# The ends of three attentions reordered: high splits ahead of the copies, and group norms one group at a time

## The reference, cut to what matters

```python
ya = neighborhood_attention(qa, ka, va, rpb_na[l])
yb = sliding_window_attention(qb, kb, vb, sink_sw[l], t5_table)
yc = axial_attention(qc, kc, vc, gq_ax[l], gk_ax[l])
ga, gb, gc = split_cols(g_group[l], GROUP_WIDTHS)
y = jnp.concatenate([rms_norm_2(ya, ga), rms_norm_2(yb, gb), rms_norm_2(yc, gc)], axis=-1)
x = x + gt_a * (y @ w_o[l])
```

## Time and profile before

| | us |
|---|---|
| runs, median of 3 | 2042.83 (2037.96 to 2043.96) |
| profiled execution, its time | 2036.57 |
| its span | 2034.4 |
| TensorE busy | 1886.8 |
| VectorE busy | 1638.9 |
| ScalarE busy | 1137.1 |
| mean granted TensorE clock | 0.977 of full speed |

### The profile page before, as it was taken

One profiled execution on the slowest core, in us unless ns is written; L12 is line 12 of the kernel. 1 busy time (PEld: TensorE's weight loads), 2 busy tenths in 40 slices (PEclk: granted clock), 3 DMA queues, 4 the chain that ended last, 5 costly groups with the idle time before them and its releaser, 6 DMA issues.

```text
span 2034.4 us, 29285 instructions
## 1 busy us (share of the span) xinstructions
PE 1886.8 (93%) x9222; PEld 1560.4 (77%) x9222; DVE 1638.9 (81%) x2173; ACT 1137.1 (56%) x1616; POOL 36.1 (2%) x47
## 2 busy tenths in 40 slices
PE   1999999978899999999999999988799999789998
PEld 1987888867788888888888888866678887577886
DVE  6988886768898999998998989897776669677554
ACT  1435444443777777777777777654544444544443
POOL 2000000000000000000000000000000000000000
PEclk9999999989999999999999999988899999889999
DMA  8877996556699999999999999957468875745662
GB/s 293 338 256 272 346 362 213 150 167 213 201 364 339 368 335 372 330 353 349 343 356 340 363 340 363 337 192 223 139 211 269 272 245 149 249 136 178 217 218 73
DMA packets 368507, 551.08 MB, mean 271 GB/s; under 512 B 35860, under 2 KB 293143, under 8 KB 368375
## 3 DMA queue, kind: packets, MB, share of 16 engines
q1 hardware_dynamic: 365424, 547.81, 80.5%
q10 hardware_dynamic: 2118, 1.46, 0.3%
q0 software_dynamic: 832, 0.30, 0.1%
HBM read 548.38 MB, written 1.08 MB: 270 GB/s over the span
## 4 chain that ended last, share of the span: by engine, by line
PE 81%; DVE 11%; ACT 4%; issue 2%; DMA 2%; POOL 0%; SPq 0%; DVEq 0%; ACTq 0%; POOLq 0%
PE ps L402 24%; PE ps L404 24%; PE ps L403 23%; PE ps L891 2%; DVE units_low L397 2%; ACT prob L1253 2%; PE ps L1060 2%; PE ps L945 2%; DVE mod_acc L1561 1%; PE ps L878 1%; ACT units_high L393 1%; DVE x_tokens L1588 1%; DVE x_normed L1587 1%; DMA mod_in<-in_mod_w 1%; DMA mod_in<-in_w_mod 1%
## 5 line engine op out<-in xcount | busy, mean ns | idle before, releaser
L397 DVE TENSOR_TENSOR units_low<-raw_units,units_high 128x1024 fp32r<-128x1024 f32 (+2 forms) x840 | 982.8, 1220 | 113.4 <-ACT units_high L393 107.3
L393 ACT ACTIVATE units_high<-raw_units 128x1024 fp32r<-128x1024 f32 (+2 forms) x840 | 844.8, 1058 | 237.7 <-PE ps L404 217.8
L402 PE MATMUL ps<-units_high,hT_high 128*128 128x512 f32 (+2 forms) x1576 | 621.8, 395 | 8.3 <-DVE hT_low L1630 3.8
L404 PE MATMUL ps<-units_high,hT_low 128*128 128x512 f32 (+2 forms) x1576 | 617.5, 392 | 0.0
L403 PE MATMUL ps<-units_low,hT_high 128*128 128x512 f32 (+2 forms) x1576 | 614.1, 390 | 0.0
L402 PEld LDWEIGHTS ps<-units_high,hT_high 128*128 128x128 f32 (+1 forms) x1576 | 296.9, 188 | 75.0 <-issue 5.8
L404 PEld LDWEIGHTS ps<-units_high,hT_low 128*128 128x128 f32 (+1 forms) x1576 | 296.4, 188 | 66.0
L403 PEld LDWEIGHTS ps<-units_low,hT_high 128*128 128x128 f32 (+1 forms) x1576 | 296.6, 188 | 63.8 <-issue 0.2
L402 PE MATMUL ps<-units_high,aT_high 128*128 128x512 f32 x632 | 258.8, 409 | 1.2 <-DVE qkT L1798 0.6
L404 PE MATMUL ps<-units_high,aT_low 128*128 128x512 f32 x632 | 248.2, 393 | 0.0
L403 PE MATMUL ps<-units_low,aT_high 128*128 128x512 f32 x632 | 246.5, 390 | 0.0
(11 more groups left out here) (275 smaller groups left out, 1438.7 us busy)
## 6 DMA issues: line engine op xcount, KB each, us to landing
raw_units<-in_moe_w_gate SPq DMA_DIRECT2D x352, 256.0 KB, 4.6
raw_units<-in_moe_w_up SPq DMA_DIRECT2D x352, 256.0 KB, 5.8
raw_units<-in_moe_w_down SPq DMA_DIRECT2D x176, 512.0 KB, 6.4
mod_in<-in_mod_w SPq DMA_DIRECT2D x96, 512.0 KB, 5.8
mod_in<-in_w_mod SPq DMA_DIRECT2D x96, 512.0 KB, 5.3
raw_units<-in_w_gu SPq DMA_DIRECT2D x176, 256.0 KB, 3.5
raw_units<-in_w_down SPq DMA_DIRECT2D x44, 512.0 KB, 4.3
raw_units<-in_w_in SPq DMA_DIRECT2D x32, 512.0 KB, 6.8
```

Source lines behind the costliest of these rows:

```text
L393: eng.activation(whi[:rows, n % H, 0:width], raw[:rows, n % R, 0:width], ACT.Copy).then_inc(f.hi, 1)
L397: eng.tensor_tensor(low[:rows, n % R, 0:width], raw[:rows, n % R, 0:width], whi[:rows, n % H, 0:width].bitcast(F32), ALU.subtract).then_in ...
L402: pe.matmul(dst, ah, bh, start=start, stop=False, **kw)
L404: return pe.matmul(dst, al, bh, start=False, stop=stop, **kw)
```

## The change

It has two parts. In all three attentions ScalarE's high split of an output-weight unit moves from behind the copies of a pair to ahead of them. In the second and third attention the end is done group by group: the sink's exponential and the squares of the third group (heads 10 to 15) are put between the last pair's exponentials and its copies; heads 10 to 15 are scaled first, then 0 to 7, then 8 and 9; the roots of the first and third group are made in one chain, those of the middle group in a second one; the chunks of y are transposed in the order 0 1, 6 7, 2 3, 4 5, the last two pairs only behind the second unit of the projection, and the output weights are loaded in that order. TensorE waits for heads 10 to 15 to be scaled before it makes the product of head 8, which lies in the same PSUM bank.

```diff
@@ -438,6 +438,9 @@
     GROUPS = ((0, 256), (256, 640), (640, 1024))
+    G_AT = (0, 4, 2)
+    Y_PAIRS = [(0, 1, 2, 3, 4), (0, 3, 1, 2), (0, 3, 1, 2)]
+    Y_CHUNK = lambda a, c: 2 * Y_PAIRS[a][c // 2] + c % 2
 
@@ -566,7 +569,7 @@
                 bias_load(1 + l, nth)
-            phase(fb, n0 + N_WO2, 8, rows_of(g["w_o_2"][l]))
+            phase(fb, n0 + N_WO2, 8, lambda k: rows_of(g["w_o_2"][l])(Y_CHUNK(1 + l, k)))
             mods(HEAD_MODS[1 + l][0] + HEAD_MODS[1 + l][1])
@@ -768,6 +771,8 @@
 
+            if free is not None:
+                pe.wait_ge(*free)
             for k in range(chunks):
@@ -780,6 +785,8 @@
                     sum_gate(0)
+                if beside is not None and k == 1:
+                    beside()
             for t in range(T):
@@ -880,6 +887,8 @@
                     pe.wait_ge(s_pte, i0 + j + 1)
+                    if second and j == n - 2:
+                        pe.wait_ge(s_ho, 6 * (a - 1) + 2)
                     h = order[j]
@@ -893,16 +902,15 @@
 
-        def y_transposes(a):
+        def y_transposes(a, first, end):
 
             w = KR if a == 0 else P
-            chunks = W1 // KR if a == 0 else DC
-            for pair in range(chunks // 2):
+            for pair in range(first, end):
                 pe.wait_ge(s_y, Y_BEFORE[a] + Y_READY[a][pair])
                 if pair >= 4:
                     pe.wait_ge(s_yTl, 2 * YT0[a] + 2)
                 for i in range(2):
-                    c = 2 * pair + i
+                    c = Y_CHUNK(a, 2 * pair + i)
                     for t in range(T):
@@ -1140,8 +1148,9 @@
             attention(1 + l)
-            y_transposes(1 + l)
-            project_out(fb, n0 + N_WO2, DC, P, lambda k: (s_yTl, 2 * YT0[1 + l] + k + 1))
+            y_transposes(1 + l, 0, 2)
+            project_out(fb, n0 + N_WO2, DC, P, lambda k: (s_yTl, 2 * YT0[1 + l] + k + 1),
+                        free=(s_ho, 6 * (l + 1)), beside=lambda: y_transposes(1 + l, 2, 4))
             sum_cols(s + 1)
@@ -1253,6 +1262,10 @@
                                              bias=negm(qt, h), scale=-1.0, accum_out=sums(qt, h))
                     last.then_inc(s_exp, 1)
+                if p < AHEAD:
+                    split_high(ac, f, n_out + p, 0, rows)
+                if p == (n - 1) // 2 and ending is not None:
+                    ending()
                 for j in pair:
                     ac.wait_ge(s_ptp, i0 + j + 1)
@@ -1260,8 +1273,6 @@
                                   ps[:, 6 + j % 2, 0:w], ACT.Copy).then_inc(s_pte, 1)
-                if p < AHEAD:
-                    split_high(ac, f, n_out + p, 0, rows)
 
@@ -1465,18 +1475,26 @@
             transposed(3, 7)
-            attention(1 + l, fb, n0 + N_WO2)
-
-            ac.wait_ge(s_al, 2 + l)
-            ac.activation(ale[:, :, 0:6], ale[:, :, 0:6], ACT.Exp).then_inc(s_ale, 1)
-            for nth, (out_of, t, grp) in enumerate(((1, 0, 0), (2, 1, 0), (3, 0, 1), (3, 0, 2), (4, 1, 1))):
+            def group_square(t, grp, scaled):
                 c0, c1 = GROUPS[grp]
-                ac.wait_ge(s_ho, 4 * l + out_of)
-                ac.activation(qkT[:, 4 + 2 * nth:6 + 2 * nth, :].rearrange("p a b -> p (a b)")[:, 0:c1 - c0],
-                              xn[:, t, c0:c1], ACT.Square, scale=(c1 - c0) ** -0.5, accum_out=ssx[:, 0, 2 * grp + t:2 * grp + t + 1])\
-                    .then_inc(s_gsq, 1)
-            yT_high(1 + l)
-            highs(fb, n0 + N_WO2, AHEAD, 8)
+                ac.wait_ge(s_ho, 6 * l + scaled)
+                ac.activation(qkT[:, 4 * grp + 2 * t:4 * grp + 2 * t + 2, :].rearrange("p a b -> p (a b)")[:, 0:c1 - c0],
+                              xn[:, t, c0:c1], ACT.Square, scale=(c1 - c0) ** -0.5,
+                              accum_out=ssx[:, 0, G_AT[grp] + t:G_AT[grp] + t + 1]).then_inc(s_gsq, 1)
+
+            def sink_and_last_group():
+                ac.wait_ge(s_al, 2 + l)
+                ac.activation(ale[:, :, 0:6], ale[:, :, 0:6], ACT.Exp).then_inc(s_ale, 1)
+                for t in range(T):
+                    group_square(t, 2, 1 + t)
+
+            attention(1 + l, fb, n0 + N_WO2, ending=sink_and_last_group)
+            group_square(1, 0, 4)
+            group_square(0, 1, 5)
+            yT_high(1 + l, 0, 4)
+            highs(fb, n0 + N_WO2, AHEAD, AHEAD + 2)
+            yT_high(1 + l, 4, 8)
+            highs(fb, n0 + N_WO2, AHEAD + 2, 8)
             highs(fb, n0 + N_FFN2, 0, 3)
@@ -2131,20 +2148,51 @@
             link(ve.reciprocal(ale[:, :, :], xstat[:, 1, :, :]))
-            heads_out(1 + l, s_ho)
-            ve.wait_ge(s_ho, 4 * (l + 1))
-            c0, c1 = GROUPS[2]
-            link(ve.tensor_tensor_reduce(out=qkT[:, 0:2, :].rearrange("p a b -> p (a b)")[:, 0:c1 - c0],
-                                         in0=xn[:, 1, c0:c1], in1=xn[:, 1, c0:c1], scale=1.0 / (c1 - c0), scalar=0.0,
-                                         op0=ALU.mult, op1=ALU.add, accum_out=ssx[:, 0, 5:6]))
-            ve.wait_ge(s_gsq, 5 * (l + 1))
-            link(ve.tensor_scalar(ssx[:, 0, 0:6], ssx[:, 0, 0:6], EPS, None, ALU.add))
-            rsqrt(ssx[:, 0, 0:6], ssx[:, 1, 0:6], ssx[:, 2, 0:6], ssx[:, 3, 0:6])
-            for i, (c0, c1) in enumerate(GROUPS):
+
+            def heads_scaled(h0, h1):
+                last = max(HEAD_ORDER.index(h) for h in range(h0, h1))
+                ve.wait_ge(s_pv, HEADS_BEFORE[1 + l] + 1 + last)
                 for t in range(T):
-                    ve.tensor_scalar(xn[:, t, c0:c1], xn[:, t, c0:c1], ssx[:, 1, 2 * i + t:2 * i + t + 1], None,
-                                     ALU.mult).then_inc(s_y, 1)
-            yT_low(1 + l)
+                    at = (h0 % 8) * HD
+                    ve.tensor_tensor(
+                        xn[:, t, h0 * HD:h1 * HD].rearrange("p (h d) -> p h d", d=HD),
+                        ps[:, 2 * t + h0 // 8, at:at + (h1 - h0) * HD].rearrange("p (h d) -> p h d", d=HD),
+                        ale[:, t, h0:h1][:, :, None].broadcast_to((P, h1 - h0, HD)), ALU.mult).then_inc(s_ho, 1)
+
+            def group_square(t, grp):
+                c0, c1 = GROUPS[grp]
+                return ve.tensor_tensor_reduce(
+                    out=qkT[:, 4 * grp + 2 * t:4 * grp + 2 * t + 2, :].rearrange("p a b -> p (a b)")[:, 0:c1 - c0],
+                    in0=xn[:, t, c0:c1], in1=xn[:, t, c0:c1], scale=1.0 / (c1 - c0), scalar=0.0,
+                    op0=ALU.mult, op1=ALU.add, accum_out=ssx[:, 0, G_AT[grp] + t:G_AT[grp] + t + 1])
+
+            def group_roots(a, b):
+                link(ve.tensor_scalar(ssx[:, 0, a:b], ssx[:, 0, a:b], EPS, None, ALU.add))
+                rsqrt(ssx[:, 0, a:b], ssx[:, 1, a:b], ssx[:, 2, a:b], ssx[:, 3, a:b])
+
+            def group_normed(grp):
+                c0, c1 = GROUPS[grp]
+                for t in range(T):
+                    at = G_AT[grp] + t
+                    ve.tensor_scalar(xn[:, t, c0:c1], xn[:, t, c0:c1], ssx[:, 1, at:at + 1], None, ALU.mult)\
+                        .then_inc(s_y, 1)
+
+            heads_scaled(10, 16)
+            heads_scaled(0, 8)
+            ve.wait_ge(s_ho, 6 * l + 4)
+            link(group_square(0, 0))
+            ve.wait_ge(s_gsq, 4 * l + 3)
+            group_roots(0, 4)
+            group_normed(0)
+            heads_scaled(8, 10)
+            ve.wait_ge(s_ho, 6 * l + 6)
+            link(group_square(1, 1))
+            group_normed(2)
+            yT_low(1 + l, 0, 2)
+            ve.wait_ge(s_gsq, 4 * l + 4)
+            group_roots(4, 6)
+            group_normed(1)
+            yT_low(1 + l, 2, 4)
             for k in range(AHEAD, 8 + 3):
```

More of the change, by code:

```diff
@@ L756, in conv_in, with project_out @@
                 last.then_inc(fa.used, 1)
-        def project_out(f, n0, chunks, rows, ready, conv=False):
+        def project_out(f, n0, chunks, rows, ready, conv=False, free=None, beside=None):
             yTh, yTl = (v[:, :, :, :].rearrange("p a k s -> p (a k) s") for v in (aTh, aTl))
@@ L1015, in _ @@
         attention(0)
-        y_transposes(0)
+        y_transposes(0, 0, 5)
         project_out(fa, N_WO1, W1 // KR, KR, lambda k: (s_yTl, k + 1))
@@ L1239, in swiglu, with attention @@
                     hooks[j]()
-        def attention(a, f, n_out, rows=P):
+        def attention(a, f, n_out, rows=P, ending=None):
             second = a > 0
@@ L1272, in _, with yT_high @@
         YP0 = YT0
-        def yT_high(a):
+        def yT_high(a, first, end):
             w = KR if a == 0 else P
-            chunks = W1 // KR if a == 0 else DC
-            for c in range(chunks):
+            for c in range(first, end):
                 ac.wait_ge(s_yTp, YP0[a] + c // 2 + 1)
@@ L1282, in yT_high @@
                 else:
-                    gcol = V_GG + 8 * (a - 1) + c
+                    gcol = V_GG + 8 * (a - 1) + Y_CHUNK(a, c)
                     ac.activation(hTh[0:w, c, :], src, ACT.Copy, scale=cols[:, gcol:gcol + 1]).then_inc(s_yTh, 1)
@@ L1358, in _ @@
```

(9 more changed lines are left out.)

## The result

The changed kernel takes 2024.8 us (median of 4 runs, 2022.54 to 2026.55), the kernel before 2040.39 beside it (4 runs, 2037.84 to 2043.96): ratio 0.9922, 95% interval 0.9899 to 0.9944, 15.6 us faster between the medians. I forecast 2035.0 with a range from 2028.5: the side was right, the size half of what came. The profiled execution took 2026.55, 10.0 less than that of before. Single executions of one kernel differ by up to 13 us here, so times are compared by medians and ratios, and the profiles stretch by stretch.

The account below looks back on a forecast made before the run. The prediction took TensorE's dense products to bound most of the kernel, a serial chain the head-pair loops, and VectorE and TensorE almost level the end. Terms -12.4 and +4.6 gave -7.8, so 2035.0 us from 2042.83; range 2028.5 to 2041.5.

Parts of the forecast that it names:

- Part 1: Attention loops: the high split goes into ScalarE's idle time before the copies, 0.95 us sooner per pair; sum -12.4 us.
- rival (a): End of second and third attention: TensorE's clock stays up, tail costs 0.3 us instead of 2.4; total -11.9; chance 0.2.
- rival (d): Attention loops: more pairs run at half clock, 1.5 us dearer each; at eleven, +8.7, 2051.5 us; chance 0.07.
- The first pairs: Start of the loops: full 0.95 us gain in the first attention, nothing in the second, half in the third.
- Part 2: End of second and third attention by groups: projection 3.5 us sooner, residual 2.4 later (2.2 in the third); sum +4.6 us.
- (b): End of attentions: clock stays low through units 0 and 1, residual 5.2 us late; total -2.2, 2040.6 us; chance 0.13.
- (c): Attention loops: VectorE's maxima set the pace, part 1 gains perhaps half, 6.2 us; total -1.6, 2041.2 us; chance 0.1.
- The scale: Whole kernel: profiled 2036.57 us gave 2028.8; three timed runs' median, 2042.83, lay 6.3 above, so the forecast was 2035.0.

Follow-up runs that it names:

- e0: The changed kernel run again, nothing altered, against the kernel before: median 2024.31 us, ratio 0.9922.
- e2: The changed kernel with the high split put back behind the copies, leaving the end by groups alone: median 2044.30 us, ratio 1.0017 to the kernel before.
- e10: The changed kernel with the split put back behind the copies in the first attention alone: median 2031.91 us, ratio 0.9953 to the kernel before.
- e5_before_bridged: The kernel before, no split moved, with four extra products in TensorE's pause before a pair's transposes: median 2032.57 us, ratio 0.9970 to the kernel before.
- e1: The kernel before with nothing but the high split moved ahead of the copies: median 2023.57 us, ratio 0.9915 to the kernel before.
- e4: The changed kernel with two low splits and two modulation sums ahead of the second half of y's low parts: 2015.69 us, ratio 0.9881 to the kernel before.
- e6: e4 with eight extra products on TensorE between the scores of the first and second pair: median 2015.80 us, ratio 0.9892 to the kernel before.
- e7: e4 with extra products in TensorE's last two pauses of the second and third attention: median 2013.51 us, ratio 0.9877 to the kernel before.
- e8: e4 with the extra products of both e6 and e7: median 2012.14 us, ratio 0.9865 to the kernel before.
- e3: The changed kernel with one low split and one modulation sum ahead of the second half of y's low parts: 2019.02 us, ratio 0.9906 to the kernel before.

## Why the prediction was right or wrong

- **Part 1, -12.4: wrong in size, -17.3 measured.** The step that failed is "The difference, 0.95, is the split's place in the queue", taken as all that a moved split gives. The queue's share is right where it can be seen alone (81.2 to 72.7 us for nine splits). But I treated the clock of the loop as given. The earlier trace rows had it, 0.70 and a pair of 7.63 us, and I used them only against rival (a) and for rival (d), in which the clock gets worse; "Shorter pairs make TensorE denser, which speaks against it" was the start of the missing rival, in which it gets better. What the runs showed in its place: the move also keeps TensorE's clock up in the loops, and filling the pause alone, with no split moved, is worth 6.1 (3.5 to 8.6).
- **The first pairs** gave less than I counted: 12.4 less the 8.5 of the stretches is 3.9 for the first two pairs, and the seven profiles with the split ahead and nothing else changed there average 35.4 us (31.9 to 38.2) against 37.4 with it behind (36.9, 38.3, 37.2), about 2.0 with a scatter that is larger. 8.5 + 2.0 + 6.1 = 16.6 for 17.3 measured.
- **Part 2, +4.6: right in mechanism, +3.5 measured** (0.6 to 6.3). In the second attention each mark of the tail was hit within 0.7 us. What I had not counted is the half clock in the norm's transposes behind the residual (3.65 against 1.94); what I had counted too dear is the residual itself: over six old tails in the profiles it starts at +34.9 to +36.4 (mean 35.8), and I had only one, at +35.34, to compare with. Up to the feed-forward's input the six old tails take 45.8 on average and eight new ones with VectorE's order as changed and no extra products (two each of after, e0, e2 and e10) 47.4, so 1.6 a tail, 3.2 for two.
- **Rival (a)** did not happen in the second attention and in neither of e0_after's: products there start at 0.43. In the profile of the changed kernel the third attention had the clock up at its last pair (first product at +11.55, residual at +35.2), though its first products too start at 0.43. Made to happen, it gives 5.7 us for the two tails by the ratios (3.7 between the medians); I had 4.1. The rule of the Trainium skill that I cited there, TensorE: Matmul & The Clock Gate, "Why this matters for your kernels", asks for short pauses between bursts of matmuls. In direction the loop's rows agree (pauses of at most 0.7 us, with one of 1.03 in each first attention: 1.00 in every stretch; up to 1.6: 0.77 to 0.94), and I had weighed the rule only for the tail. But the section warns of pauses longer than these 1.6, so by it alone the loops before would have kept their clock; the measurement decides.
- **Rivals (b), (c), (d)** did not come: unit 1 runs at 0.23, VectorE waits before its maxima, and no loop stretch got slower.
- **The scale.** 2035.0 came from a median of 2042.83 of three runs. Over 17 runs it is 2039.8. That is 3 of the 10.2 us by which I missed; the other 7 are the sum, 5 of them part 1 and 1 part 2, and the last lies within what the runs can tell.

## What to carry to other kernels

Where a loop's profile shows TensorE's clock between its two levels, a change that shortens TensorE's pauses can get two gains, as here, the queue's and the clock's; price the second from the rows at either level, and give it a chance of its own as a gain. Before costing such a change, fill the pause with products whose result is not used: it costs one run and measures the clock's share with nothing moved. When work is started sooner on one engine, look at what the list of the other holds between the new waits: here reordering four operations was worth more (8.4) than the regrouping cost.

## What was unexpected of the hardware

- In the loop, with a pause of up to 1.6 us in each pair of 5.2 or 6.1, the clock was down part of the time, a different part in each execution (0.77, 0.87, 0.93 for the same stretch of the same instructions), while with the split ahead, and pauses of at most 0.7 (one of 1.03 in each first attention), all 29 such stretches of ten profiles show 1.00 and last 21.3 or 25.7 us to 0.02. Whether the scatter in time of the kernel before (2036.55 to 2046.95) comes from this isn't shown, and two things speak against its being all of it: e5_before_bridged scatters as much (2029.57 to 2039.81) with 1.00 in its profiled loops, and the first exponentials of the first attention, ahead of which no kernel differs, begin anywhere from 433.1 to 437.3 in the thirteen profiles.
- Behind the residual, TensorE's pause before the norm's transposes was 1.49 us in the ten tails of before, e5, e1, e4 and e6, and the 16 transposes took 1.94 each time. After pauses of 2.22 or 2.23 (e7, e8) they took 1.94 in three tails and 3.29 in the fourth, after 2.62 and 2.63 (e3) 3.32 and 3.50, after 4.94 to 4.97 (ten tails) 3.47 to 3.65. That is why taking VectorE's low splits sooner is worth more than the residual's own microseconds: in e4's second attention the residual starts 3.6 sooner than in the changed kernel, and the feed-forward's input is there 4.1 sooner.
